# Differential attention: the output factor from two logarithms on ScalarE, and two passes of the next scores ahead of the ninth key tile's transpose

## The chip, the cores and the metric

The kernel runs on one core of a Trainium2 chip. The metric is the device time of one execution in microseconds; of several runs the median is taken. The profile comes from one profiled execution on that core.

## The reference, cut to what matters

The program is one step of a two-layer backbone. Layer 0 mixes tokens by a Fourier transform, layer 1 by differential attention; both are followed by a gated output projection. The change touches only the attention of the 1024 latent tokens over 1152 keys, for eight heads with two score maps each:

```python
s = einsum('bqhcd,bkhcd->cbhqk', q, k) * scale
p = softmax(s, axis=-1)
a = p[0] - lam * p[1]
o = einsum('bhqk,bkhv->bqhv', a, v)
o = rms_norm(o, subln) * (1.0 - lam_init)      # over the 256 values of a head
out = (o * silu(g)) @ w_out
```

The two softmax sums of a query row are `lsum[0]` and `lsum[1]`. The kernel doesn't divide the first map by its sum. It forms `e0 + ratio * e1`, with `ratio = -lam * lsum[0] / lsum[1]`, multiplies by the values, and puts 1/`lsum[0]` into a factor of each row: rsqrt(mean of squares + eps) / `lsum[0]`.

## The kernel before

**Tiles.** A step is one block of 128 queries of one head: eight steps for each head, 64 in all (four pairs of heads, `STEPS` = 16 steps for each pair). The query and key data are held as a high and a low part, so that each product is made in three passes (high times high, high times low, low times high), in the order of `passes`. The 1152 keys are three chunks of 384 columns. The scores of half 0 (map 0) lie in PSUM banks 0 to 2 and those of half 1 (map 1) in banks 3 to 5. Bank 6 (`TURN`) receives transposes of the combined weights. Bank 7 (`OB`) holds the output in its first 256 columns and the output's transpose in the other 256.

**Rotations.** `rotations` calls `rotate(pair, m_, last)` once for each step and twice more at the end, on TensorE, ScalarE and VectorE alike. Numbered through, they are rotations 0 to 65. In rotation r four steps are in work: `now` is step r, `ahead` is r+1, `back` is r-1 and `back2` is r-2. Each engine runs its own list in a fixed order, and semaphores tie the lists together. `GROUPS` cuts the nine key tiles of 128 keys into 0 to 3, 4 to 7, and the ninth alone.

**TensorE in a rotation.** `scores(now, 1)` (nine matmuls of 384 columns, L2588); `turn(back, 0)` (four transposes, L2602), which waits for the combined weights; `scores(ahead, 0)`, with `turn_o(back2)` (two transposes of the normalised output, L2632) before its third pass; `turn(back, 1)`; `apply(back, 0)` (twelve matmuls of 256 columns, L2621); `turn(back, 2)`, a single transpose; `apply(back, 1)` (twelve) and `apply(back, 2)` (three). The last of these raises `av_done`. Since there is one `TURN` bank, each `turn` waits until VectorE has read the group before:

```python
pe.wait_ge(at_lo_done, NG * (STEPS * i + m) + n + 1)
```

`apply(back, n)` waits for `at_lo_done` of its own group. `scores` waits until the exponential of the same half of the step before has been taken, since that exponential reads the same banks (`expd`).

**ScalarE in a rotation.** `mean_square(back2)`: a Square over the output bank with a running sum (writes `a_junk`, L2705), its accumulator read, a logarithm into `olog` (L2708), and an Exp with scale -0.5 into `orstd` (L2711). It waits for `av_done`. Then `normalise(back2)` (writes `a_on`, L2718), which waits for `factor`; `high_half(back, 0)` (`a_at_hi`, L2695); `exponential(now, 1)` (`a_e`, L2686, and its accumulator read); `high_half(back, 1)`; `high_half(back, 2)`; `exponential(ahead, 0)`.

**VectorE in a rotation.** `scale_factor(back2)` (`ofac` = `orstd` times `linv`, L2807); `maximum(now, 1)` (L2766); `low_half(back, 0)` (`a_at_lo`, L2776, which waits for the high half of the same group); `gate(back2)` (L2819); `weigh(now)` (reciprocals `linv`, L2786, and the ratio, L2788); `low_half(back, 1)`; `maximum(ahead, 0)`; `low_half(back, 2)`; `combine(now)` (L2798).

**Ends.** In rotation 63 there is no `ahead`; VectorE there combines before the ninth tile's low half. Rotations 64 and 65 drain the pipeline and mix in the first products of the output projection (`held`, L254). SyncE loads the heads' tiles and waits for `av_done` once for each head before it overwrites them.

Of the kernel before, what the change touches and what calls it, by code (L numbers as in the profile page):

```python
# [10 lines left out]
ALU = mybir.AluOpType  # L11
ACT = mybir.ActivationFunctionType
AX = mybir.AxisListType

P = 128
# [2439 lines left out]
def attention(nc, sh, keys_in, g_d, y_d, ahead, following, ps):  # L2455
# [8 lines left out]
    with ExitStack() as ctx:  # L2464
        def sb(name, shape, dt=F32):
            return ctx.enter_context(nc.sbuf_tensor(f"a_{name}", shape, dt))
# [14 lines left out]
        sb("heads", [P, 162304 // 4])  # L2481

        nmax, lsum, linv = (sb(n, [P, 2, 2]) for n in ("nmax", "lsum", "linv"))
        ratio, osum, olog, orstd, ofac = (sb(n, [P, 2]) for n in ("ratio", "osum", "olog", "orstd", "ofac"))
        TURN, OB, LAST_OB = 6, 7, 5

        following.begin(nc, sh, 1)
# [15 lines left out]
        av_done = sem("av_done")  # L2503
        squared = sem("squared")
        logged = sem("logged")
        rooted = sem("rooted")
        factor = sem("factor")
        on_done = sem("on_done")
        o_turned = sem("o_turned")
# [58 lines left out]
        @block.tensor  # L2568
        def _(pe):

            def scores(at_step, half, turn_between=None):
                if at_step is None:
                    if turn_between is not None:
                        turn_between()
                    return
                i, m = at_step
                s, t = m // QT, m % QT
                if t == 0:

                    pe.wait_ge(qk_in[s][half], 96 * i + 96)  # L2580

                pe.wait_ge(expd, 2 * (STEPS * i + m) + half + 1)
                tok = slice(t * P, (t + 1) * P)
                for j, (a, x) in enumerate(passes(*(x[:, half, tok] for x in q[s]), *(x[:, half, :] for x in k[s]))):
                    if j == 2 and turn_between is not None:
                        turn_between()
                    for c in range(NCH):
                        mm = pe.matmul(ps[:, 3 * half + c, 0:CH], a, x[:, c * CH:(c + 1) * CH],  # L2588
                                       start=(j == 0), stop=(j == 2))
                mm.then_inc(score, 1)  # L2590

            def rotate(pair, m_, last):
                def turn(at_step, n):
                    if at_step is None:
                        return
                    i, m = at_step
                    if n == 0:
                        pe.wait_ge(combined, STEPS * i + m + 1)

                    pe.wait_ge(at_lo_done, NG * (STEPS * i + m) + n + 1)  # L2600
                    for j, kt in enumerate(GROUPS[n]):
                        mm = pe.transpose(ps[:, TURN, j * P:(j + 1) * P], e[:, m % 2, 0, kt * P:(kt + 1) * P], sh.ident[:, :])  # L2602
                    mm.then_inc(turned, 1)

                def apply(at_step, n):

                    if at_step is None:
                        return
                    i, m = at_step
                    s = m // QT  # L2610
                    if n == 0:
                        if m % QT == 0:
                            pe.wait_ge(v_in[s], 64 * i + 64)
                        if out_bank(at_step) == OB:
                            pe.wait_ge(gated, STEPS * i + m + 1)

                    pe.wait_ge(at_lo_done, NG * (STEPS * i + m) + n + 2)
                    for kt in GROUPS[n]:
                        for j, (a, x) in enumerate(passes(at_hi[:, kt, :], at_lo[:, kt, :],
                                                          v[s][0][:, kt, :], v[s][1][:, kt, :])):  # L2620
                            mm = pe.matmul(ps[:, out_bank(at_step), 0:UC], a, x, start=(kt == 0 and j == 0),  # L2621
                                           stop=(kt == TT - 1 and j == 2))
                    if n == NG - 1:
                        mm.then_inc(av_done, 1)

                def turn_o(at_step):
                    if at_step is None:
                        return
                    i, m = at_step
                    pe.wait_ge(on_done, STEPS * i + m + 1)  # L2630
                    for h in range(2):
                        mm = pe.transpose(ps[:, out_bank(at_step), UC + h * P:UC + (h + 1) * P], on[:, m % 2, h * P:(h + 1) * P], sh.ident[:, :])  # L2632
                    mm.then_inc(o_turned, 1)

                now, ahead = step(pair, m_, last), step(pair, m_ + 1, last)
                back, back2 = step(pair, m_ - 1, False), step(pair, m_ - 2, False)
                if last and m_ > STEPS:
                    back = None
                def held(e, ds):

                    if e == 0:
                        pe.wait_ge(expd, 2 * (H // 2) * STEPS + 2)
                    pe.wait_ge(following.ahead_lo, 2 * e + 1)
                    pe.wait_ge(following.y_lo_done, e + 1)
                    for d in ds:
                        following.products(pe, ps, d, e)

                scores(now, 1)
                turn(back, 0)
                if last and m_ == STEPS:  # L2650
                    turn_o(back2)
                    turn(back, 1)
                    apply(back, 0)
                    turn(back, 2)
                    apply(back, 1)
                    apply(back, 2)
                    held(0, following.HELD)
                    return
                if last and m_ > STEPS:
                    turn_o(back2)  # L2660
                    held(1, following.HELD)
                    return
                scores(ahead, 0, lambda: turn_o(back2))
                turn(back, 1)
                apply(back, 0)
                turn(back, 2)
                apply(back, 1)
                apply(back, 2)

            scores((0, 0), 0)  # L2670
            rotations(pe, rotate)

        @block.scalar
        def _(act):
# [5 lines left out]
            def rotate(pair, m_, last):  # L2680
# [17 lines left out]
                def mean_square(at_step):  # L2698

                    if at_step is None:  # L2700
                        return
                    i, m = at_step
                    s, n = m % 2, STEPS * i + m + 1
                    act.wait_ge(av_done, n)
                    act.activation(junk[:, :], ps[:, out_bank(at_step), 0:UC], ACT.Square, scale=linv[:, s, 0:1],  # L2705
                                   accum_out=osum[:, s:s + 1]).then_inc(squared, 1)
                    act.wait_ge(squared, n)
                    act.activation(olog[:, s:s + 1], osum[:, s:s + 1], ACT.Ln, bias=sh.eps[:, 0:1],  # L2708
                                   scale=1.0 / UC).then_inc(logged, 1)
                    act.wait_ge(logged, n)  # L2710
                    act.activation(orstd[:, s:s + 1], olog[:, s:s + 1], ACT.Exp, scale=-0.5).then_inc(rooted, 1)  # L2711

                def normalise(at_step):
                    if at_step is None:
# [27 lines left out]
                high_half(back, 0)  # L2742
                exponential(now, 1)
                high_half(back, 1)
                if last and m_ == STEPS - 1:
                    following.ahead_w_hi(act, 0)
                high_half(back, 2)
# [10 lines left out]
        def _(dve):  # L2758
            def rotate(pair, m_, last):
# [38 lines left out]
                    dve.scalar_tensor_tensor(e[:, s, 0, 0:KEYS], e[:, s, 1, 0:KEYS], ratio[:, s:s + 1],  # L2798
                                             e[:, s, 0, 0:KEYS], ALU.mult, ALU.add).then_inc(combined, 1)

                def scale_factor(at_step):
                    if at_step is None:
                        return
                    i, m = at_step
                    s, n = m % 2, STEPS * i + m + 1
                    dve.wait_ge(rooted, n)
                    dve.tensor_tensor(ofac[:, s:s + 1], orstd[:, s:s + 1], linv[:, s, 0:1], ALU.mult).then_inc(factor, 1)  # L2807

                def gate(at_step):

                    if at_step is None:
# [13 lines left out]
                    back = None  # L2825
                if last and m_ == STEPS:
                    low_half(back, 0)
                    scale_factor(back2)
                    gate(back2)
                    following.first_y_lo(dve, 0)  # L2830
                    low_half(back, 1)
                    following.ahead_w_lo(dve, 1)
                    low_half(back, 2)
                    following.first_y_lo(dve, 1)
                    return
                if last and m_ > STEPS:
                    scale_factor(back2)
                    following.w_lo(dve, 0, following.LATE_D)
                    gate(back2)
                    following.w_lo(dve, 1, following.LATE_D)  # L2840
                    return
                scale_factor(back2)
                maximum(now, 1)
                low_half(back, 0)
                gate(back2)
# [254 lines left out]
```

## Time and profile before

| | |
|---|---|
| median of 3 runs | 2166.29 us (2162.74 to 2167.59) |
| the profiled execution's own time | 2163.82 us |
| its span, first to last instruction | 2162.0 us |
| TensorE busy | 2103.3 us, 97% |
| VectorE busy | 1392.5 us, 64% |
| ScalarE busy | 907.9 us, 42% |
| mean granted TensorE clock | 0.991 of full speed |

The span is what the trace covers; the execution's own time is 1.8 us longer. Busy time is a sum over all stages. A busy TensorE in the profile isn't TensorE at its peak, since the records of matmuls overlap and their ends are modelled; short gaps are best read from the starts of instructions. Of transposes and matmuls merged into one row (x3, x4) the start is that of the first. An idle time in square brackets names what ended it.

### The profile page before, as it was taken

Reading aid. Unit: us, or ns where it says so; the run is one execution under the profiler, and the core shown is the slowest. Engines: PE = TensorE matmul, PEld = TensorE weight load, DVE = VectorE, ACT = ScalarE, POOL = GpSimd, SP = SyncE. Lnnn points to the kernel's source line nnn. Section 1 sums busy time; section 2 is a strip of 40 time slices with the busy share of each in tenths; the row PEclk is TensorE's granted clock in tenths of the full one; section 3 lists DMA queues with packets and bytes.
Section 4 is the critical chain, followed back from the end, with each engine's and each line's share of the span. In section 5 each row is a group of like instructions: output and inputs, shape, how many; then the busy total and the mean of one; then the engine's idle time right before and its main releaser. Section 6 shows DMA issues by size and latency. Waiting matters only on the chain. (4 is left out here: it accounts for less than half of the span.)

```text
span 2162.0 us, 33133 instructions
## 1 busy us (share of the span) xinstructions
PE 2103.3 (97%) x13347; PEld 2029.5 (94%) x13347; DVE 1392.5 (64%) x2126; ACT 907.9 (42%) x1674; POOL 1.6 (0%) x8
## 2 busy tenths in 40 slices
PE   6999999989999999999999999999999999999997
PEld 4999977989999999999999999989999999989997
DVE  7986864764258888888655322248888888875223
ACT  7321243232124333433433333346666666664220
POOL 0000000000000000000000000000000000000000
PEclk9999999989999999999999999999999999999998
DMA  8653442784234544555454544471344443207332
GB/s 333 210 180 122 151 149 101 251 315 157 68 126 150 163 147 145 158 151 156 151 181 151 217 161 161 142 268 40 139 166 166 166 160 132 114 1 268 106 128 88
DMA packets 125974, 342.69 MB, mean 159 GB/s; under 512 B 14464, under 2 KB 69888, under 8 KB 116608
## 3 DMA queue, kind: packets, MB, share of 16 engines
q1 hardware_dynamic: 125824, 340.61, 45.5%
q8 instruction: 105, 1.72, 0.3%
q14 instruction: 45, 0.37, 0.1%
HBM read 225.70 MB, written 114.82 MB: 157 GB/s over the span
## 5 line engine op out<-in xcount | busy, mean ns | idle before, releaser
L254 PE MATMUL o_ps<-o_y_hi,o_w 128*128 128x384 f32 x768 | 197.9, 337 | 9.9 <-DVE o_y_lo L2352 9.2
L254 PE MATMUL a_ps<-o_y_hi,o_w 128*128 128x384 f32 x768 | 196.4, 335 | 1.2 <-DVE o_x_early L2360 0.7
L2686 ACT ACTIVATE a_e<-a_ps,a_nmax 128x1152 f32<-128x1152 f32 x127 | 155.3, 1223 | 62.9 <-DVE a_nmax L2766 62.9
L2621 PE MATMUL a_ps<-a_v_hi,a_at_hi 128*128 128x256 f32 x576 | 173.1, 301 | 0.0
L2766 DVE TENSOR_REDUCE a_nmax<-a_ps 128x1 f32<-128x1152 f32 x127 | 171.7, 1352 | 0.2 <-PE a_ps L2588 0.2
L2621 PE MATMUL a_ps<-a_v_lo,a_at_hi 128*128 128x256 f32 x576 | 162.7, 282 | 0.0
L2621 PE MATMUL a_ps<-a_v_hi,a_at_lo 128*128 128x256 f32 x576 | 162.4, 282 | 0.0
L254 PEld LDWEIGHTS o_ps<-o_y_hi,o_w 128*128 128x128 f32 x768 | 140.5, 190 | 10.6 <-DVE o_y_lo L2352 9.3
L254 PEld LDWEIGHTS a_ps<-o_y_hi,o_w 128*128 128x128 f32 x768 | 138.9, 188 | 2.0 <-DVE o_x_early L2360 1.1
L2352 DVE TENSOR_TENSOR o_y_lo<-o_y_raw,o_y_hi 128x384 fp32r<-128x384 f32 x94 | 51.2, 555 | 134.1 <-ACT o_y_hi L2301 134.0
L254 PE MATMUL o_ps<-o_y_lo,o_w 128*128 128x384 f32 x384 | 129.4, 337 | 0.0
L254 PE MATMUL a_ps<-o_y_lo,o_w 128*128 128x384 f32 x384 | 128.3, 334 | 0.0
L1133 PE MATMUL p_ps<-p_late_hi,p_w_lo 128*128 128x384 f32 x384 | 128.3, 334 | 0.0
L1133 PE MATMUL p_ps<-p_late_hi,p_w_hi 128*128 128x384 f32 x384 | 128.3, 334 | 0.0
L1133 PE MATMUL p_ps<-p_late_lo,p_w_hi 128*128 128x384 f32 x384 | 128.3, 334 | 0.0
L2695 ACT CAST a_at_hi<-a_ps 128x512 fp32r<-128x512 f32 (+1 forms) x192 | 91.7, 478 | 75.2 <-PE a_ps L2602 75.0
L2621 PEld LDWEIGHTS a_ps<-a_v_hi,a_at_hi 128*128 128x128 f32 x576 | 113.3, 197 | 0.0
L1601 DVE TENSOR_TENSOR p_v_lo<-p_ps,p_v_hi 128x256 fp32r<-128x256 f32 x72 | 30.5, 424 | 126.7 <-ACT p_v_hi L1401 126.0
L2776 DVE TENSOR_TENSOR a_at_lo<-a_ps,a_at_hi 128x512 fp32r<-128x512 f32 (+1 forms) x192 | 105.7, 551 | 8.5 <-ACT a_at_hi L2695 1.3
L2621 PEld LDWEIGHTS a_ps<-a_v_lo,a_at_hi 128*128 128x128 f32 x576 | 109.9, 191 | 0.0
L1205 PE MATMUL p_ps<-p_w_hi,p_h_hi 128*128 128x256 f32 x384 | 109.7, 286 | 0.0
L2621 PEld LDWEIGHTS a_ps<-a_v_hi,a_at_lo 128*128 128x128 f32 x576 | 109.6, 190 | 0.0
(370 smaller groups left out, 5771.0 us busy)
## 6 DMA issues: line engine op xcount, KB each, us to landing
p_w_raw<-w_in_dram SPq DMA_DIRECT2D x32, 1024.0 KB, 4.8
o_y_raw<-y_dram SPq DMA_DIRECT2D x96, 192.0 KB, 3.5
g_wada<-w_ada_dram SPq DMA_DIRECT2D x32, 512.0 KB, 4.5
f_w_raw<-w_u_dram SPq DMA_DIRECT2D x32, 512.0 KB, 4.4
o_w_raw<-w_out_dram SPq DMA_DIRECT2D x28, 512.0 KB, 4.8
g_dram<-g_stage SPq DMA_DIRECT2D x16, 576.0 KB, 3.2
f_g<-g_dram SPq DMA_DIRECT2D x8, 1152.0 KB, 7.7
y_dram<-f_y SPq DMA_DIRECT2D x8, 1152.0 KB, 5.6
```

The source lines that it names most:

```text
L254: mm = pe.matmul(ps[:, d, 0:CH], a, m, start=(e == 0 and j == 0), stop=(e == ET - 1 and j == 2))
L1133: mm = pe.matmul(ps[:, bank, 0:CH], a, x, start=(first and i == 0 and j == 0), stop=(stop and i == len(left) - 1 and j == 2), skip_group_c ...
L1205: mm = pe.matmul(ps[:, 4 * p + at % 3, 0:UC], a, x, start=(d == 0 and m == 0), stop=(d == DT - 1 and m == 2))
L1601: dve.tensor_tensor(v_lo[:, t, :], ps[:, 4 * p + at % 3, 0:UC], v_hi[:, t, :].bitcast(F32), ALU.subtract).then_inc(drained[p], 1)
L2352: dve.tensor_tensor(y_lo[:, e, :], y_raw[:, k % NR, :], y_hi[:, e, :].bitcast(F32), ALU.subtract).then_inc(y_lo_done, 1)
L2621: mm = pe.matmul(ps[:, out_bank(at_step), 0:UC], a, x, start=(kt == 0 and j == 0), stop=(kt == TT - 1 and j == 2))
L2686: act.activation(split3(e[:, m % 2, half, :]), ps[:, 3 * half:3 * half + 3, 0:CH], ACT.Exp, bias=nmax[:, m % 2, half:half + 1], scale=1.0, ...
L2695: act.copy(at_hi[:, tiles[0]:tiles[-1] + 1, :].rearrange("p a b -> p (a b)"), ps[:, TURN, 0:len(tiles) * P]).then_inc(at_hi_done, 1)
L2766: dve.tensor_reduce(nmax[:, m % 2, half:half + 1], ps[:, 3 * half:3 * half + 3, 0:CH], AX.XY, ALU.max, negate=True).then_inc(maxed, 1)
L2776: dve.tensor_tensor(into, ps[:, TURN, 0:len(tiles) * P], hi, ALU.subtract).then_inc(at_lo_done, 1)
```

## The change

Two edits in attention, and nothing outside it.

The output factor was the product of `orstd` = exp(-0.5 * olog) and `linv`, made on VectorE. Now ScalarE takes a second logarithm, `llog` = ln(`linv`), in a new function `inverse_log(now)` between `high_half(back, 1)` and `high_half(back, 2)`, a step's own rotation. `mean_square` two rotations later writes `ofac` itself as exp(-0.5 * olog + llog). VectorE's `scale_factor` is gone. `normalise` still waits for `factor`, which ScalarE now raises.

`scores` gets an argument for the passes to make. The first two passes of the second half of the next step move from the start of the next rotation to the place between `apply(back, 0)` and `turn(back, 2)` of this one; the third pass stays at the start of the rotation. Before the rotations the first step's two passes are issued too.

```diff
-            def scores(at_step, half, turn_between=None):
+            def scores(at_step, half, which=(0, 1, 2), turn_between=None):
...
-                pe.wait_ge(expd, 2 * (STEPS * i + m) + half + 1)
+                if which[0] == 0:
+                    pe.wait_ge(expd, 2 * (STEPS * i + m) + half + 1)
...
+                    if j not in which:
+                        continue
...
-                mm.then_inc(score, 1)
+                if which[-1] == 2:
+                    mm.then_inc(score, 1)
...
-                scores(now, 1)
+                scores(now, 1, (2,))
                 turn(back, 0)
...
-                scores(ahead, 0, lambda: turn_o(back2))
+                scores(ahead, 0, turn_between=lambda: turn_o(back2))
                 turn(back, 1)
                 apply(back, 0)
+                scores(ahead, 1, (0, 1))
                 turn(back, 2)
                 apply(back, 1)
                 apply(back, 2)
 
             scores((0, 0), 0)
+            scores((0, 0), 1, (0, 1))
             rotations(pe, rotate)
...
                     act.wait_ge(logged, n)
-                    act.activation(orstd[:, s:s + 1], olog[:, s:s + 1], ACT.Exp, scale=-0.5).then_inc(rooted, 1)
+                    act.wait_ge(inv_logged, n)
+                    act.activation(ofac[:, s:s + 1], olog[:, s:s + 1], ACT.Exp, bias=llog[:, s:s + 1], scale=-0.5).then_inc(factor, 1)
+
+                def inverse_log(at_step):
+
+                    if at_step is None:
+                        return
+                    i, m = at_step
+                    s, n = m % 2, STEPS * i + m + 1
+                    act.wait_ge(inv_done, n)
+                    act.activation(llog[:, s:s + 1], linv[:, s, 0:1], ACT.Ln).then_inc(inv_logged, 1)
...
                 high_half(back, 1)
+                inverse_log(now)
...
                 high_half(back, 2)
...
-                def scale_factor(at_step):
-                    if at_step is None:
-                        return
-                    i, m = at_step
-                    s, n = m % 2, STEPS * i + m + 1
-                    dve.wait_ge(rooted, n)
-                    dve.tensor_tensor(ofac[:, s:s + 1], orstd[:, s:s + 1], linv[:, s, 0:1], ALU.mult).then_inc(factor, 1)
...
-                scale_factor(back2)
                 maximum(now, 1)
                 low_half(back, 0)
```

## Rows read from the trace of the kernel before

**Rows 1.** Busy time by stretch, clock and DMA share, two stretches of attention.

```profile
core 0: us, PE busy (x) PEld busy (x) DVE busy (x) ACT busy (x) POOL busy (x), PEclk, DMA share, GB/s
1600.00:1700.00 100.00, 100.00 (x719) 95.10 (x718) 80.86 (x129) 69.19 (x156) 0.00 (x0) 1.00 0.29 105
...
1900.00:1940.00 40.00, 36.42 (x267) 34.08 (x266) 31.15 (x53) 27.17 (x63) 0.00 (x0) 1.00 0.00 1
```

**Rows 2.** Waits in attention: who waited for whom, us, times, longest.

```profile
PEld a_ps L2602 <- DVE a_at_lo L2776: 12.4, 65, 1.2
```

**Rows 3.** Timeline of one rotation: start us, duration us, engine, line, operation.

```profile
1600.15 0.69 PE L2588 MATMUL a_ps<-a_k_hi,a_q_hi 128*128 128x384 f32 x3
...
1600.65 0.47 ACT L2705 ACTIVATE a_junk<-a_ps,a_linv 128x256 f32<-128x256 f32 x1
...
1601.23 0.30 ACT L2708 ACTIVATE a_olog<-a_osum,eps 128x1 f32<-128x1 f32 x1
...
1601.56 0.20 ACT L2711 ACTIVATE a_orstd<-a_olog 128x1 f32<-128x1 f32 x1
...
1601.72 0.60 PE L2602 MATMUL a_ps<-ident,a_e 128*128 128x128 f32 x4
...
1601.99 0.47 ACT L2718 ACTIVATE a_on<-a_ps,a_ofac 128x256 f32<-128x256 f32 x1 [0.23 <-DVE a_ofac L2807]
...
1602.36 0.58 ACT L2695 CAST a_at_hi<-a_ps 128x512 fp32r<-128x512 f32 x1
...
1603.19 0.68 DVE L2776 TENSOR_TENSOR a_at_lo<-a_ps,a_at_hi 128x512 fp32r<-128x512 f32 x1
...
1603.31 1.22 ACT L2686 ACTIVATE a_e<-a_ps,a_nmax 128x1152 f32<-128x1152 f32 x1 [0.37 <-DVE a_nmax L2766]
...
1603.95 0.64 PE L2602 MATMUL a_ps<-ident,a_e 128*128 128x128 f32 x4
...
1604.34 0.36 PE L2621 MATMUL a_ps<-a_v_hi,a_at_hi 128*128 128x256 f32 x1
...
1605.73 0.28 PE L2621 MATMUL a_ps<-a_v_hi,a_at_lo 128*128 128x256 f32 x1
...
1605.99 0.33 PE L2602 MATMUL a_ps<-ident,a_e 128*128 128x128 f32 x1
...
1606.36 0.27 ACT L2695 CAST a_at_hi<-a_ps 128x128 fp32r<-128x128 f32 x1 [1.14 <-PE a_ps L2602]
...
1607.12 0.28 DVE L2776 TENSOR_TENSOR a_at_lo<-a_ps,a_at_hi 128x128 fp32r<-128x128 f32 x1
...
1607.31 1.41 DVE L2798 SCALAR_TENSOR_TENSOR a_e<-a_e,a_ratio 128x1152 f32<-128x1152 f32 x1
...
1607.83 0.28 PE L2621 MATMUL a_ps<-a_v_hi,a_at_lo 128*128 128x256 f32 x1
```

**Rows 4.** Timeline, two other rotations: where the wait in question is open.

```profile
1446.63 0.59 ACT L2695 CAST a_at_hi<-a_ps 128x512 fp32r<-128x512 f32 x1 [0.73 <-PE a_ps L2602]
...
1447.25 0.69 DVE L2776 TENSOR_TENSOR a_at_lo<-a_ps,a_at_hi 128x512 fp32r<-128x512 f32 x1
...
1930.69 0.68 DVE L2776 TENSOR_TENSOR a_at_lo<-a_ps,a_at_hi 128x512 fp32r<-128x512 f32 x1
...
1931.43 0.66 PE L2602 MATMUL a_ps<-ident,a_e 128*128 128x128 f32 x4 [0.98 <-DVE a_at_lo L2776]
...
1931.84 0.36 PE L2621 MATMUL a_ps<-a_v_hi,a_at_hi 128*128 128x256 f32 x1
```

**Rows 5.** Timeline: last output product and the square that waits for it.

```profile
1942.61 0.28 PE L2621 MATMUL a_ps<-a_v_hi,a_at_lo 128*128 128x256 f32 x1
...
1942.93 0.47 ACT L2705 ACTIVATE a_junk<-a_ps,a_linv 128x256 f32<-128x256 f32 x1 [1.12 <-PE a_ps L2621]
```

**Rows 6.** Timeline: TensorE's start of rotations 2 and 63.

```profile
1452.02 0.69 PE L2588 MATMUL a_ps<-a_k_hi,a_q_hi 128*128 128x384 f32 x3
...
1927.65 0.69 PE L2588 MATMUL a_ps<-a_k_hi,a_q_hi 128*128 128x384 f32 x3
```

More of the change, by code:

```diff
@@ L2483, in attention @@
         nmax, lsum, linv = (sb(n, [P, 2, 2]) for n in ("nmax", "lsum", "linv"))
-        ratio, osum, olog, orstd, ofac = (sb(n, [P, 2]) for n in ("ratio", "osum", "olog", "orstd", "ofac"))
+        ratio, osum, olog, llog, ofac = (sb(n, [P, 2]) for n in ("ratio", "osum", "olog", "llog", "ofac"))
         TURN, OB, LAST_OB = 6, 7, 5
@@ L2505, in attention @@
         logged = sem("logged")
-        rooted = sem("rooted")
+        inv_logged = sem("inv_logged")
         factor = sem("factor")
@@ L2577, in scores @@
                 s, t = m // QT, m % QT
-                if t == 0:
+                if t == 0 and which[0] == 0:
                     pe.wait_ge(qk_in[s][half], 96 * i + 96)
-                pe.wait_ge(expd, 2 * (STEPS * i + m) + half + 1)
+                if which[0] == 0:
+                    pe.wait_ge(expd, 2 * (STEPS * i + m) + half + 1)
                 tok = slice(t * P, (t + 1) * P)
                 for j, (a, x) in enumerate(passes(*(x[:, half, tok] for x in q[s]), *(x[:, half, :] for x in k[s]))):
+                    if j not in which:
+                        continue
                     if j == 2 and turn_between is not None:
@@ L2836, in rotate @@
                 if last and m_ > STEPS:
-                    scale_factor(back2)
                     following.w_lo(dve, 0, following.LATE_D)
@@ L2841, in rotate @@
                     return
-                scale_factor(back2)
                 maximum(now, 1)
```

## The prediction

> **What bounds the kernel now.** I read the page first: TensorE is busy for 97% of the span, VectorE for 64%, ScalarE for 42%. So the place to look is attention as TensorE sees it. The stretches [rows 1] show TensorE busy for all of 100 us in the middle of the stage, at the full granted clock, which is the 2.4 GHz level, with VectorE at 81% and ScalarE at 69%. The starts of rotations 2 and 63 [rows 6] are 475.63 us apart, so a rotation takes 475.63 / 61 = 7.80 us. Next, the waits [rows 2]: the weight load of a transpose waits 12.4 us in 65 cases for VectorE's low half, 0.19 us a rotation. The timeline of one rotation [rows 3] shows where. `apply(back, 0)` starts its twelfth matmul at 1605.73. Its twelve take starts 0.12 us apart (1.39 us for eleven spacings, a little more behind the transposes), so the ninth tile's transpose could start at 1605.85, but it starts at 1605.99. TensorE loses 0.14 us in each rotation there, and this is the only loss that repeats. Bare of it, TensorE's own list is 7.66 us.
>
> The reader should see one more thing in the same rows, a loop through three engines. ScalarE's Square waits for the last output product (`av_done`). Behind it on ScalarE, in order, stand the logarithm, the Exp, `a_on`, and only then the high half of group 0. VectorE's low half of group 0 follows, and `turn(back, 1)` waits for that. From there TensorE runs on to the last output product of the rotation, which releases the next Square. No wait is put down to this loop now. It has slack, and the change puts two passes into it.
>
> **The change, the loop first.** Old loop, from the start of a Square to the start that the next could have, all from starts and ends of [rows 3] unless said:
> - Square at 1600.65 to `a_on` at 1601.99: 1.34 us.
> - `a_on` to the high half of group 0: 0.37, and its duration 0.58.
> - High half's end to low half: 0.03 where VectorE was free (1447.22 to 1447.25, [rows 4]). Low half: 0.68.
> - Low half's end to a transpose that waits: 0.06 (1931.37 to 1931.43, [rows 4]). From this transpose's start to the first product: 0.41 [rows 4].
> - Twelve products: 1.39 + 0.12 = 1.51.
> - Ninth transpose to the last product's start: 1605.99 to 1607.83, 1.84.
> - Last product's start to the Square that waits for it: 0.32 (1942.61 to 1942.93, [rows 5]).
>
> Sum: 1.34 + 0.37 + 0.58 + 0.03 + 0.68 + 0.06 + 0.41 + 1.51 + 1.84 + 0.32 = 7.14 us. Against 7.80 it has 0.66 us of slack, and that is why the Square now starts 0.50 us after its rotation without anyone noticing.
>
> **The moved passes.** Three passes take 1.57 us (1600.15 to 1601.72, [rows 3]), two take 1.05. They used to lie between the last output product and `turn(back, 0)`, outside the loop. Now they lie between `apply(back, 0)` and `turn(back, 2)`, inside it. TensorE does the same number of matmuls. Their banks are free: the exponential of half 1 ends at 1604.53 and its accumulator read closely behind [rows 3], and they would start at 1605.85. In this place they cover the 0.14 us wait, so TensorE's own list falls to 7.66 us. But the loop grows by 1.05.
>
> **The factor.** Removed: VectorE's product and the hop to it and back. From the Exp's start to `a_on`'s start is 0.43 us now (1601.56 to 1601.99). In its place the Exp alone stands in front of `a_on`, with a wait on its own engine as between the logarithm and the Exp now, which is 0.33 from start to start with a duration of 0.30, so 0.03 over the duration. The new Exp takes its bias from a tile. Two durations stand near: 0.30 (the logarithm, which has a bias tile) and 0.20 (the Exp, which has none). I take 0.30, since the operands are then the same kind: 0.33 to `a_on`, a gain of 0.10. With 0.20 it would be 0.23, a gain of 0.20; that is one bound. The other: the second wait ahead of the Exp, for `inv_logged`, is met a rotation early, but if passing it costs as much again as a hop from VectorE to TensorE (0.06, [rows 4]) the gain is 0.04. The Trainium skill (ScalarE: Activation LUTs, section What ACT_TABLE_LOAD costs) says that each per-partition pointer operand adds about 93 ns to an ACTIVATE, whatever the function. By that rule the 0.09 us between the two rows is the bias and not the function, and the sum goes with 0.30; if it were the function, the sum would be that of the low bound. The trace before has no Exp of one column with a bias, so it can't decide.
>
> The second logarithm costs 0.20 to 0.30 us on ScalarE between two high halves, where ScalarE sits idle for 1.14 us before the ninth tile's high half [rows 3]. `linv` is done by then: its reciprocal waits for the same exponential as the high half of group 1, which runs 0.59 us. So it costs nothing. Without that cover it would cost its 0.3. VectorE's 0.16 us is freed in front of its first maximum, which waits for the scores anyway: nothing.
>
> **New loop:** 7.14 + 1.05 - 0.10 = 8.09 us. It is longer than TensorE's 7.66, so it sets the period, and TensorE waits 8.09 - 7.66 = 0.43 us at `turn(back, 1)` for the low half of group 0, in place of 0.14 at `turn(back, 2)`. What else is late? The combine. The ninth transpose goes 0.91 us later against what precedes it. High half after 0.37 with 0.27, hop 0.03, low half to combine 0.19, combine 1.41, hop 0.06: 2.33 us from the ninth transpose to `turn(back, 0)`. TensorE needs 1.84 + 0.12 + 0.52 = 2.48. So it is just hidden, by 0.15, and 0.43 of waiting follows behind it. SyncE's loads wait for `av_done` and the output store for the gate, both later by the same drift as their users; the transfers take 0.29 of 100 us [rows 1], and no engine waits for them in attention.
>
> **The sum.** Rotation 1 hands over 1.05 - 0.14 = 0.91 us later. Rotations 2 to 62 are 61 rotations with 8.09 - 7.80 = 0.29 more: 17.9. Rotation 63 has no `ahead`. There the loop is open already: `turn(back, 1)` starts 1931.43 - 1927.65 = 3.78 us after the rotation [rows 4, 6]. In the new kernel the Square starts 0.20 after the rotation (the 0.32 less a spacing of 0.12), and 1.24 + 0.37 + 0.58 + 0.03 + 0.68 + 0.06 bring it to 3.16: 0.62 back. The rest is unchanged. 0.91 + 17.9 - 0.62 = 18.2 us. The profiled execution (2163.8) would become 2182.0. The median of the runs shown is 2.5 us above it, so 2166.3 + 18.2 = 2184.5.
>
> Bounds: with the short Exp the period is 8.00 (8.09 less 0.10, rounded up for the hops), 0.20 more than now, and the sum 12.5: 2178.8. With 0.06 more in the loop the sum is 21.8: 2188. If the high half of group 0 couldn't start before `a_on` has ended (it starts 0.10 before that end now), 0.10 more: 24, 2190.
>
> **Rivals.**
> 1. *Only TensorE's list counts: the ninth transpose no longer waits and the loop doesn't bite.* For it: the only repeating wait of TensorE in the trace vanishes [rows 2, 3], and the hop through VectorE goes too. Then the period is 7.66: 0.91 - 61 x 0.14 = -7.6, and with rotation 63 back 0.62, about -8: 2158. Against it: this needs the loop to be 0.43 us shorter than I sum it. The kernel gets faster from 0.29 shorter on. All ten terms are read from rows, most repeat in each rotation, and none has 0.3 us of room but the Exp, which has 0.1. Chance 5%.
> 2. *The two cancel: within 0.2%.* The period would have to be within 0.07 us of 7.80, so the loop 0.22 to 0.36 too long in my sum. Chance 6%.
> 3. *The short Exp*: 2178.8, slower still by 0.6%. Chance 14%.
> 4. *A longer loop or a second wait*: the combine comes later than its margin of 0.15, or the double wait costs more than 0.06. Each 0.1 us in the loop is 6 us. 2190 and more, chance 7%.
> 5. *The clock falls because TensorE waits in each rotation.* In the stretch at the end [rows 1] it sat idle 3.6 of 40 us, 9%, against 5% here, and the granted clock stayed 1.00. Chance 2%; it would be far above the range.
>
> My forecast, the loop at 8.09, has 66%.
>
> **Numbers.** 0.2% is 4.3 us and is about what a measurement can tell from no change. Slower by more: 66 + 14 + 7 + 2 = 89%. Same 6%, faster 5%. The range from 2176.5 to 2191 takes in the short Exp, the loop 0.1 longer, and the 2 us by which the median stands off single runs; it leaves out cases 1, 2 and 5 and the tail of 4.
>
> **What the profile after would show.** A period near 8.09 us between starts of rotations. TensorE's transposes L2602 waiting for VectorE's low half about 61 times with 0.4 us, in front of four transposes and not in front of one. The Square waiting for the last output product in each rotation, where it did once. The Exp at 0.30 us, and 0.33 from it to `a_on`. The second logarithm without an idle time behind it that wasn't there. The low half of group 0 waiting for ScalarE instead of following the maximum. The prediction is wrong if the Square doesn't wait for the product, or if `turn(back, 1)` starts without a wait: then the loop is shorter than summed.

## The result and the profile after

| | before | after |
|---|---|---|
| median | 2165.8 us (4 runs) | 2183.3 us (2182.1 to 2184.4, 4 runs) |
| span of the profiled execution | 2162.0 us | 2180.0 us |

The changed kernel is slower, by 0.8%: the ratio is 1.0082, with a 95% interval from 1.0069 to 1.0094, or 17.5 us between the medians. I had put it at 2184.5 us, in a range from 2176.5 to 2191.

One rotation of the changed kernel from its timeline (start, duration, engine, line, operation; the functions are the same ones under new line numbers: L2591 scores, L2606 turn, L2625 apply, L2711 to L2718 Square, logarithm and factor, L2734 `a_on`, L2701 high half, L2793 low half, L2815 combine):

```profile
1600.09 0.69 PE L2591 MATMUL a_ps<-a_k_hi,a_q_lo 128*128 128x384 f32 x3
...
1600.29 0.48 ACT L2711 ACTIVATE a_junk<-a_ps,a_linv 128x256 f32<-128x256 f32 x1 [0.31 <-PE a_ps L2625]
...
1600.89 0.30 ACT L2714 ACTIVATE a_olog<-a_osum,eps 128x1 f32<-128x1 f32 x1
...
1601.22 0.30 ACT L2718 ACTIVATE a_ofac<-a_olog,a_llog 128x1 f32<-128x1 f32 x1
...
1601.55 0.48 ACT L2734 ACTIVATE a_on<-a_ps,a_ofac 128x256 f32<-128x256 f32 x1
...
1601.92 0.58 ACT L2701 CAST a_at_hi<-a_ps 128x512 fp32r<-128x512 f32 x1
...
1602.27 0.77 PE L2591 MATMUL a_ps<-a_k_hi,a_q_lo 128*128 128x384 f32 x3
...
1602.53 0.69 DVE L2793 TENSOR_TENSOR a_at_lo<-a_ps,a_at_hi 128x512 fp32r<-128x512 f32 x1 [0.36 <-ACT a_at_hi L2701]
...
1603.28 0.66 PE L2606 MATMUL a_ps<-ident,a_e 128*128 128x128 f32 x4 [0.24 <-DVE a_at_lo L2793]
...
1603.69 0.36 PE L2625 MATMUL a_ps<-a_v_hi,a_at_hi 128*128 128x256 f32 x1
...
1605.21 0.69 PE L2591 MATMUL a_ps<-a_k_hi,a_q_hi 128*128 128x384 f32 x3
...
1606.26 0.27 PE L2606 MATMUL a_ps<-ident,a_e 128*128 128x128 f32 x1
...
1607.07 1.41 DVE L2815 SCALAR_TENSOR_TENSOR a_e<-a_e,a_ratio 128x1152 f32<-128x1152 f32 x1
...
1608.03 0.28 PE L2625 MATMUL a_ps<-a_v_hi,a_at_lo 128*128 128x256 f32 x1
...
1608.15 0.69 PE L2591 MATMUL a_ps<-a_k_hi,a_q_lo 128*128 128x384 f32 x3
...
1608.36 0.48 ACT L2711 ACTIVATE a_junk<-a_ps,a_linv 128x256 f32<-128x256 f32 x1 [0.31 <-PE a_ps L2625]
...
1608.68 0.60 PE L2606 MATMUL a_ps<-ident,a_e 128*128 128x128 f32 x4
```

What the reader is to see, against [rows 3]:
- From Square to Square it is 1608.36 - 1600.29 = 8.07 us, where [rows 6] gave 7.80.
- TensorE's last output product starts at 1608.03 and the Square 0.33 behind it. In the kernel before the Square came 0.50 after its rotation's start, and 0.62 after the product (1600.03).
- `turn(back, 1)` at 1603.28 starts 1.01 us after the third pass ahead of it (1602.27). In the kernel before it was 0.61 (1603.34 to 1603.95), with no wait. So it stands 0.40 us, and it starts 0.06 after the low half's end (1602.53 + 0.69).
- The ninth transpose at 1606.26 doesn't wait any more.
- The combine ends at 1608.48 and `turn(back, 0)` starts at 1608.68, which is when the third pass is through: hidden, with 0.14 to spare.

The waits from 1453 to 1945, the steady rotations (who waited for whom: us in total, times, longest):

```profile
ACT a_junk L2711 <- PE a_ps L2625: 18.7, 61, 0.3
...
DVE a_at_lo L2793 <- ACT a_at_hi L2701: 63.6, 183, 0.4
...
PE a_ps L2606 <- DVE a_at_lo L2793: 14.5, 61, 0.2
```

The Square waits for the last product 61 times, once in each steady rotation; it did so once in the whole kernel before. The transposes wait for the low half 61 times. The 14.5 us of matmul idle understate this wait, since the profile counts the matmul ahead as busy to its modelled end; the starts give 0.40 each.

TensorE's start of rotations 2 and 63 of the changed kernel, and of `turn(back, 1)` in rotation 63:

```profile
1454.91 0.69 PE L2591 MATMUL a_ps<-a_k_hi,a_q_lo 128*128 128x384 f32 x3
...
1946.95 0.69 PE L2591 MATMUL a_ps<-a_k_hi,a_q_lo 128*128 128x384 f32 x3
...
1950.14 0.66 PE L2606 MATMUL a_ps<-ident,a_e 128*128 128x128 f32 x4 [0.76 <-DVE a_at_lo L2793]
```

(1946.95 - 1454.91) / 61 = 8.07 us a rotation: 16.4 us more than the 475.63 of [rows 6]. From the start of rotation 63 to that transpose it is 3.19 us, where it was 3.78.

### The profile page after: what moved, and what is told of

It reads as the page before. It is cut to its first block and busy times, and to the rows that moved or that the text cites. A ratio compares the mean times of both kernels' runs of the same rounds, so it can differ in the third digit from the quotient of the medians.

```text
span 2180.0 us, 33197 instructions
## 1 busy us (share of the span) xinstructions
PE 2106.0 (97%) x13347; PEld 2024.6 (93%) x13347; DVE 1396.6 (64%) x2062; ACT 917.2 (42%) x1738; POOL 1.6 (0%) x8
## 5 line engine op out<-in xcount | busy, mean ns | idle before, releaser
L2625 PE MATMUL a_ps<-a_v_hi,a_at_hi 128*128 128x256 f32 x576 | 172.9, 300 | 0.0
L2625 PE MATMUL a_ps<-a_v_hi,a_at_lo 128*128 128x256 f32 x576 | 162.9, 283 | 0.0
L2625 PE MATMUL a_ps<-a_v_lo,a_at_hi 128*128 128x256 f32 x576 | 162.6, 282 | 0.0
L2701 ACT CAST a_at_hi<-a_ps 128x512 fp32r<-128x512 f32 (+1 forms) x192 | 91.7, 477 | 137.9 <-PE a_ps L2606 137.9
L2793 DVE TENSOR_TENSOR a_at_lo<-a_ps,a_at_hi 128x512 fp32r<-128x512 f32 (+1 forms) x192 | 107.2, 558 | 66.0 <-ACT a_at_hi L2701 65.9
L2606 PE MATMUL a_ps<-ident,a_e 128*128 128x128 f32 x576 | 97.8, 279 | 16.5 <-DVE a_at_lo L2793 15.3
L2625 PEld LDWEIGHTS a_ps<-a_v_hi,a_at_hi 128*128 128x128 f32 x576 | 109.9, 191 | 2.1
L2625 PEld LDWEIGHTS a_ps<-a_v_lo,a_at_hi 128*128 128x128 f32 x576 | 109.8, 191 | 0.0
```

What stands on the lines that cost most here:

```text
L2701: act.copy(at_hi[:, tiles[0]:tiles[-1] + 1, :].rearrange("p a b -> p (a b)"), ps[:, TURN, 0:len(tiles) * P]).then_inc(at_hi_done, 1)
L2793: dve.tensor_tensor(into, ps[:, TURN, 0:len(tiles) * P], hi, ALU.subtract).then_inc(at_lo_done, 1)
```

## The experiments

The edits are shown against the changed kernel, cut to the lines that matter. The times and ratios are against the kernel before, run again in the same round on the same chip: 2165.6 us for the first four runs, 2165.4 for the last three. Periods are read from two like starts in the timeline, one rotation apart; the theory that a loop through three engines sets the period is called the loop theory. The first four take the change apart.

### Only the factor

The three passes go back to the start of the rotation; the factor stays as changed.

```diff
-                scores(now, 1, (2,))
+                scores(now, 1)
...
-                scores(ahead, 1, (0, 1))
...
-            scores((0, 0), 1, (0, 1))
```

> Only the factor from two logarithms; all three passes of the second half stay at the start of the rotation. Loop theory (the chain from the last output product through Square, factor, a_on, high and low half of group 0 and back to TensorE sets the period only when passes are put into it): the period stays 7.80 us, since the loop has slack and the 0.14 us wait at the ninth transpose comes from another chain (turn of group 1, its high and low half). Time 2166, between 2163 and 2168. Rival (the ScalarE work itself costs: a second logarithm and a longer Exp, 0.3 us in each of 61 rotations): 2184, the whole of the loss.

Measured: 2166.2 us against 2165.6, ratio 1.0002 (0.9993 to 1.0011). The period is 7.79. Its wait of weight loads from 1453 to 1920, for comparison with [rows 2]:

```profile
PEld a_ps L2606 <- DVE a_at_lo L2791: 10.8, 60, 0.2
```

10.8 us in 60 cases, the 0.18 or 0.19 us each of the kernel before. So the second logarithm, the longer Exp and the lost hop are worth nothing where the loop has room, and the rival that ScalarE's work costs by itself is out.

### Only the two passes

The factor is made on VectorE again (`orstd`, then `scale_factor`), the two passes are moved.

```diff
-                    act.wait_ge(inv_logged, n)
-                    act.activation(ofac[:, s:s + 1], olog[:, s:s + 1], ACT.Exp, bias=llog[:, s:s + 1], scale=-0.5).then_inc(factor, 1)
+                    act.activation(orstd[:, s:s + 1], olog[:, s:s + 1], ACT.Exp, scale=-0.5).then_inc(rooted, 1)
...
-                inverse_log(now)
...
+                scale_factor(back2)
                 maximum(now, 1)
                 low_half(back, 0)
```

> Only the two passes moved, the factor still made on VectorE. Loop theory as summed in the prediction (the hop is worth 0.10 us): period 8.16, about 2189. Loop theory refined by the order on VectorE: the factor's product stands ahead of the first maximum there, and the low half of group 0 stands behind that maximum. From Square to low half it is then 1.15 + 0.12 + 1.27 = 2.54 us by this branch against 2.34 by the high half, so the period is about 8.35, the gain lost is 61 x 0.3, and the time about 2200 (2196 to 2204). Rival (splitting the scores costs TensorE by itself, the loop doesn't matter): no more than the changed kernel, 2183.

Measured: 2196.9 us, ratio 1.0144 (1.0128 to 1.0159). From its timeline:

```profile
1600.08 0.69 PE L2591 MATMUL a_ps<-a_k_hi,a_q_hi 128*128 128x384 f32 x3
...
1603.23 0.47 ACT L2711 ACTIVATE a_junk<-a_ps,a_linv 128x256 f32<-128x256 f32 x1 [0.31 <-PE a_ps L2625]
...
1604.15 0.20 ACT L2717 ACTIVATE a_orstd<-a_olog 128x1 f32<-128x1 f32 x1
...
1604.39 0.16 DVE L2813 TENSOR_TENSOR a_ofac<-a_orstd,a_linv 128x1 f32<-128x1 f32 x1 [1.03 <-ACT a_orstd L2717]
...
1604.46 1.35 DVE L2772 TENSOR_REDUCE a_nmax<-a_ps 128x1 f32<-128x1152 f32 x1
...
1605.73 0.68 DVE L2782 TENSOR_TENSOR a_at_lo<-a_ps,a_at_hi 128x512 fp32r<-128x512 f32 x1
...
1606.47 0.66 PE L2606 MATMUL a_ps<-ident,a_e 128*128 128x128 f32 x4 [0.39 <-DVE a_at_lo L2782]
...
1608.39 0.69 PE L2591 MATMUL a_ps<-a_k_hi,a_q_hi 128*128 128x384 f32 x3
```

The period is 1608.39 - 1600.08 = 8.31 us, near the 8.35 of the refined theory and not near 8.16. (The refinement was worked out after the result of the change was known, and before this run.) The low half (1605.73) follows the maximum, and the maximum (1604.46) follows the factor's product (1604.39), not the scores. That is the branch the refined theory names. The time lies in the refined window, 3 us under its centre and 1 above its lower end.

### One pass in place of two

```diff
-                scores(now, 1, (2,))
+                scores(now, 1, (1, 2))
...
-                scores(ahead, 1, (0, 1))
+                scores(ahead, 1, (0,))
...
-            scores((0, 0), 1, (0, 1))
+            scores((0, 0), 1, (0,))
```

> As the changed kernel, but only one pass of the next second half is moved ahead of the ninth transpose, and two stay. Loop theory: the loop is 8.07 - 0.52 = 7.55 us, below TensorE's own list of about 7.6 to 7.66 (7.80 less the 0.14 wait, and perhaps 0.07 less since the transpose's load is no longer exposed). So both kernels are beaten: the period is 7.59 to 7.68 and the time 2153 to 2159. Rival (each moved pass costs by itself, in proportion): half of the loss, 2174. Rival (the wait only moves to the next transpose): 2166.

Measured: 2156.6 us (2151.1 to 2158.6, 5 runs), ratio 0.9957 (0.9944 to 0.9971). It beats both kernels. From its timeline:

```profile
1601.70 0.69 PE L2591 MATMUL a_ps<-a_k_hi,a_q_hi 128*128 128x384 f32 x3
...
1602.24 0.27 PE L2606 MATMUL a_ps<-ident,a_e 128*128 128x128 f32 x1
...
1609.31 0.69 PE L2591 MATMUL a_ps<-a_k_hi,a_q_hi 128*128 128x384 f32 x3
```

The period is 7.61 us, and the ninth transpose comes 0.54 us behind the one pass, with no wait. TensorE shows no wait at all from 1453 to 1900, in matmuls or in weight loads. One pass is enough cover for a wait of 0.14 us and too short to make the loop the longest. Half of the move is a gain where the whole is a loss, which rules out a cost in proportion to the passes moved.

### One pass, with the old factor

> One pass moved, the factor still made on VectorE. Loop theory with VectorE's order: 8.35 - 0.52 = 7.83 us for the branch through the maximum, a hair above the 7.80 of before: 2166 to 2169, so the gain of the one pass hangs on the new factor. Loop theory without VectorE's order (hop worth 0.10): the loop is 7.65, hidden, and the time 2155 to 2160 as with the new factor.

The edit is that of one pass together with the old factor of *Only the two passes*. Measured: 2166.4 us, ratio 1.0000 (0.9991 to 1.0009). From its timeline:

```profile
1603.73 0.16 DVE L2813 TENSOR_TENSOR a_ofac<-a_orstd,a_linv 128x1 f32<-128x1 f32 x1 [0.92 <-ACT a_orstd L2717]
...
1603.81 1.35 DVE L2772 TENSOR_REDUCE a_nmax<-a_ps 128x1 f32<-128x1152 f32 x1
...
1605.08 0.68 DVE L2782 TENSOR_TENSOR a_at_lo<-a_ps,a_at_hi 128x512 fp32r<-128x512 f32 x1
...
1605.81 0.66 PE L2606 MATMUL a_ps<-ident,a_e 128*128 128x128 f32 x4
```

Product, maximum, low half and transpose follow one another without a gap: 1603.73, 1603.81, 1605.08, 1605.81. The period is 7.79, which is 8.31 less a pass of 0.52. So the one moved pass gains nothing with the old factor, and 9.6 us with the new one (2166.2 to 2156.6). Read the other way, the new factor is worth 9.8 us with one moved pass (2166.4 to 2156.6), 13.6 with two (2196.9 to 2183.3), and nothing with none.

The next three test the loop itself.

### A spare operation in the loop, with two moved passes

```diff
                     act.wait_ge(squared, n)
+                    act.activation(junk[:, :], ps[:, out_bank(at_step), 0:UC], ACT.Square, scale=linv[:, s, 0:1])
                     act.activation(olog[:, s:s + 1], osum[:, s:s + 1], ACT.Ln, bias=sh.eps[:, 0:1],
```

> The changed kernel with one more Square of 256 columns on ScalarE between the first Square and its logarithm; nobody uses what it writes. Loop theory: it adds 0.37 us (start to start of such an operation) to a loop that sets the period, so 8.07 + 0.37 = 8.44 us and 61 x 0.37 = 22.6 us: about 2206, between 2203 and 2208. Rival (ScalarE, 42% busy, has room, and what costs is TensorE's split scores): 2183, no change.

Measured: 2204.4 us, ratio 1.0181 (1.0164 to 1.0198), 21 us above the changed kernel. From its timeline:

```profile
1600.42 0.69 PE L2591 MATMUL a_ps<-a_k_hi,a_q_hi 128*128 128x384 f32 x3
...
1604.16 0.47 ACT L2714 ACTIVATE a_junk<-a_ps,a_linv 128x256 f32<-128x256 f32 x1
...
1608.84 0.69 PE L2591 MATMUL a_ps<-a_k_hi,a_q_hi 128*128 128x384 f32 x3
```

The period is 8.42 us: 0.35 more for an operation that takes 0.38 from its start to the next start and shortens the gap ahead of the logarithm a little.

### The same spare operation without moved passes

The edit is the same line, in the kernel that has only the factor.

> The same spare Square in the kernel that has the new factor but no moved pass. Loop theory: the loop has room there; the low half of group 0 is paced by the maximum ahead of it and would start at most 0.08 us later. So 2166 to 2171, at most a quarter of what the same operation costs with two moved passes. Rival (an operation on ScalarE costs its time wherever it stands): 2189.

Measured: 2170.1 us, ratio 1.0017 (1.0007 to 1.0027), 4.6 us over the kernel before. From its timeline:

```profile
1601.32 1.36 DVE L2782 TENSOR_REDUCE a_nmax<-a_ps 128x1 f32<-128x1152 f32 x1 [0.99 <-PE a_ps L2591]
...
1602.63 0.69 DVE L2792 TENSOR_TENSOR a_at_lo<-a_ps,a_at_hi 128x512 fp32r<-128x512 f32 x1
...
1609.16 1.36 DVE L2782 TENSOR_REDUCE a_nmax<-a_ps 128x1 f32<-128x1152 f32 x1 [0.99 <-PE a_ps L2591]
```

The low half starts 1.31 us after the maximum, not 1.27, and the period is 7.84, 0.05 more than with the factor alone. The same operation on the same engine costs about a fifth of what it costs in the changed kernel. It isn't quite free, since the branch by the high half (its end at 1602.60, the low half 0.03 behind) now passes the branch by the maximum by a few hundredths: TensorE's weight loads wait for the low half 120 times from 1453 to 1920, twice a rotation, and with the factor alone 60 times.

### The logarithms behind the high half

The output leaves out the RMS factor: `a_on` is scaled with `linv` alone. The logarithm and the Exp are still made, later.

```diff
                 mean_square(back2)
                 normalise(back2)
                 high_half(back, 0)
+                logarithms(back2)
                 exponential(now, 1)
...
-                    act.wait_ge(factor, STEPS * i + m + 1)
+                    act.wait_ge(squared, STEPS * i + m + 1)
...
-                                   scale=ofac[:, m % 2:m % 2 + 1]).then_inc(on_done, 1)
+                                   scale=linv[:, m % 2, 0:1]).then_inc(on_done, 1)
```

> The changed kernel, but the logarithm and the Exp of the output factor stand behind the high half of group 0, and a_on is scaled with linv alone (so the RMS factor is made and not used; this part of the computation is left out of the output). ScalarE and TensorE do the same number of operations. Loop theory: two times 0.33 us leave the loop, 8.07 - 0.66 = 7.41, below TensorE's own 7.61; the period is 7.61 to 7.66 and the time 2154 to 2159, faster than before, with the two passes still moved. Rival (the moved passes cost by where they stand on TensorE): 2183. Rival (another chain bites, above all the combine with its margin of 0.15 us): 2165 to 2180.

Measured: 2153.3 us, ratio 0.9942 (0.9925 to 0.9959), just under the expected window. From its timeline:

```profile
1599.73 0.77 PE L2591 MATMUL a_ps<-a_k_hi,a_q_hi 128*128 128x384 f32 x3
...
1600.02 0.58 ACT L2701 CAST a_at_hi<-a_ps 128x512 fp32r<-128x512 f32 x1
...
1600.49 0.30 ACT L2720 ACTIVATE a_olog<-a_osum,eps 128x1 f32<-128x1 f32 x1
...
1600.85 0.68 DVE L2802 TENSOR_TENSOR a_at_lo<-a_ps,a_at_hi 128x512 fp32r<-128x512 f32 x1
...
1607.34 0.77 PE L2591 MATMUL a_ps<-a_k_hi,a_q_hi 128*128 128x384 f32 x3
```

The period is 7.61 us. Both passes are still ahead of the ninth transpose, and TensorE makes the same matmuls in the same order as in the changed kernel. Only the two operations on ScalarE, 0.66 us, went from one side of the high half to the other, and 30 us went with them (2183.3 to 2153.3). This is the plainest evidence that the moved passes cost nothing where they stand on TensorE, and that the loop through ScalarE and VectorE is the price.

## Why the prediction was right

**The forecast's own steps, one by one.** The new loop was summed to 8.09 us and measures 8.07:

| term | predicted | measured |
|---|---|---|
| Square to `a_on` | 1.24 | 1.26 |
| `a_on` to high half, its duration | 0.95 | 0.95 |
| hop, low half, hop | 0.77 | 0.78 |
| waiting transpose to first product | 0.41 | 0.41 |
| twelve products | 1.51 | 1.52 |
| two passes | 1.05 | 1.05 |
| ninth transpose to last product | 1.84 | 1.77 |
| last product to Square | 0.32 | 0.33 |
| sum | 8.09 | 8.07 |

The one term off by more than two hundredths is the ninth transpose. A transpose that waited (0.08 to its first product, and its weight load bare) is dearer than one that didn't (0.03), so 0.05 of the 0.07 lies there. By the same effect TensorE's own list is 7.61 us and not the 7.66 that I took; it shows in the kernel with one pass.

**The Exp.** With a bias tile it takes 0.298 us, where the Exp without one took 0.203 in the kernel before. The two logarithms show the same split: 0.297 with the tile of eps, 0.208 for the new one without. So the choice of 0.30 held. The Trainium skill's rule (ScalarE: Activation LUTs, section What ACT_TABLE_LOAD costs), some 93 ns for each pointer operand (a scale or bias read from a tile of one column) and none for the function, agrees with these four numbers. The second wait ahead of the Exp cost nothing: from the logarithm to the Exp it is 0.33 us (1600.89 to 1601.22), as in [rows 3] (1601.23 to 1601.56).

**The ends.** Rotation 63 was to give back 0.62 us and gave 0.59 (3.78 to 3.19). The 61 rotations were to cost 17.9 and cost 16.4. In the profiled executions rotation 2 starts 2.89 us later than before, where the entry was to cost 0.91. To part the entry from the rest, take the time from TensorE's first attention matmul to rotation 2. The first matmul of the kernel before, of the changed kernel, and then both starts of the kernel with two passes and the spare operation and of the one with the factor alone:

```profile
1436.68 0.76 PE L2588 MATMUL a_ps<-a_k_hi,a_q_hi 128*128 128x384 f32 x3 [2.85 <-ACTq L2675]
...
1437.15 0.78 PE L2591 MATMUL a_ps<-a_k_hi,a_q_hi 128*128 128x384 f32 x3 [2.87 <-ACTq L2681]
...
1435.64 0.76 PE L2591 MATMUL a_ps<-a_k_hi,a_q_hi 128*128 128x384 f32 x3 [2.86 <-ACTq L2681]
...
1451.83 0.70 PE L2591 MATMUL a_ps<-a_k_hi,a_q_lo 128*128 128x384 f32 x3
...
1438.80 0.77 PE L2591 MATMUL a_ps<-a_k_hi,a_q_hi 128*128 128x384 f32 x3 [2.85 <-ACTq L2679]
...
1455.70 0.69 PE L2591 MATMUL a_ps<-a_k_hi,a_q_hi 128*128 128x384 f32 x3
```

It is 15.34 us before and 17.76 in the changed kernel. With the two passes moved and the clock at its full level (two passes and the spare operation) it is 16.19: the entry costs 0.85. With no pass moved but a lower clock in the first passes (the factor alone; last section) it is 16.90, 1.56 more than before. So of the 2.89 us, 0.85 belong to the change, 1.57 to the clock, and 0.47 were there when the stage began.

**Where luck had a part.** The change's own terms measure 0.85 + 16.4 - 0.59 = 16.7 us, 1.5 under the 18.2 of the sum; the medians differ by 17.5. That the spans of the two profiled executions differ by 18.0, almost the sum, is luck: the 2 us of the clock and the stage's start stand in for what the rotations fell short, and 0.7 us that went behind rotation 63 were not followed up. The margin of the combine came out at 0.14 for 0.15 with both of its sides 0.05 or 0.06 shorter than summed (2.42 and 2.28 for 2.48 and 2.33).

**What I had not seen.** One step was wrong, though the number stood. I wrote that VectorE's product of the old factor was "freed in front of its first maximum, which waits for the scores anyway: nothing", and gave the new factor 0.10 us in the loop. That holds in the kernel before: from the third pass to the maximum it is 0.72 us there (1601.20 to 1601.92), and as much with the factor alone (1604.88 to 1605.60). With the loop closed it doesn't: the old product stands ahead of the maximum, and the low half of group 0 behind it, so there was a second branch from Square to low half. In the kernel with only the passes moved it takes 1605.73 - 1603.23 = 2.50 us, against 1602.53 - 1600.29 = 2.24 by the high half in the changed kernel. The old factor costs 0.24 us a rotation there (8.31 to 8.07) and not 0.10. The slack of the old loop was less than the 0.66 that I summed, too: by the kernel with only the passes moved, the old loop was 8.31 - 1.05 = 7.26 us, which leaves 0.54 of 7.80, and one pass of 0.52 used that up. Nor does the Square's start of 0.50 us into the rotation show the slack, as I wrote: ScalarE's accumulator read for the exponential of half 0 stands right ahead of it (1600.56, then the Square at 1600.65). The forecast was spared because the changed kernel doesn't have the branch through the old product: the 7.14, 1.05 and 0.10 are all terms of the branch by the high half, which is the one that the changed kernel has. For the kernel with only the passes moved the same sum, 7.14 + 1.05 = 8.19, is 0.12 us short of the 8.31 measured.

**The rivals.** "Only TensorE's list counts" needed a loop 0.43 us shorter than summed, and 0.29 for any gain. It came true in the two kernels whose loop was cut below TensorE's list, by one pass (0.52) or by two operations (0.66). A second wait at `turn(back, 0)` was given a margin of 0.15; the trace shows 0.14, and it never opened. The clock stayed at its full level through the steady rotations with 0.40 us of waiting in each, as this stretch (busy us by engine, granted clock, DMA share) shows beside two stretches from the start of attention:

```profile
core 0: us, PE busy (x) PEld busy (x) DVE busy (x) ACT busy (x) POOL busy (x), PEclk, DMA share, GB/s
1437.00:1439.00 2.00, 1.85 (x7) 1.89 (x8) 0.00 (x0) 1.28 (x1) 0.00 (x0) 0.69 1.07 367
1439.00:1441.00 2.00, 2.00 (x8) 2.00 (x8) 1.12 (x1) 0.00 (x0) 0.00 (x0) 0.50 0.94 311
1600.00:1700.00 100.00, 96.96 (x693) 90.56 (x691) 79.14 (x112) 68.85 (x163) 0.00 (x0) 1.00 0.27 101
```

## What to carry to other kernels

When work is moved ahead of a waiting instruction to cover its wait, follow what that instruction and everything behind it releases until the chain comes back to the same engine, and add the moved work to that loop. Here a cover of 1.05 us for a gap of 0.14 made a loop with 0.5 us of slack the longest in the kernel; a cover of 0.52 gained 9 us over the kernel before, and nothing where the old factor's product still stood in the loop. Sum the new loop from its own rows through every branch, including what stands in order on each engine between two links, and choose the cover by the size of the gap and the slack left.

## What the runs showed of the hardware that I had not expected

The granted clock at the start of attention differs between executions of nearly the same program. TensorE sits idle for 2.85 us there (2.87 after). In the profile before it then runs at 1.00. In the changed kernel's profiled execution it reads 0.69 and then 0.50 in the two stretches above; 0.50 is the 1.2 GHz level, and there a pass takes 0.96 us to the next one's start in place of 0.52. Before it fell TensorE had done one pass at the full rate (0.59 us to the next) after that idle time. A stretch at or near this level stands in six of the nine profiled executions, with no order by edit that I can see (each kernel was profiled once): the mean from 1436 to 1440 was 1.00 with one pass and with two passes and the spare operation, 0.57 with the passes alone and 0.73 with the logarithms behind. The kernel with the factor alone, whose stage begins 2 us later, shows the same passes of 0.96 us. What this costs up to rotation 2 is the 1.56 us worked out above; it may be part of the 2 to 8 us by which repeated runs of one kernel differ. What decides it stays open; no run was made for it.
